# Reordering square sums, splits and copies in a two-block fp32 transformer kernel

## What is computed

```python
def first_block(x, ...):
    u = _rmsnorm(h, norm_mix_g[l])                       # first norm
    z = jnp.einsum('bsd,dn->bsn', u, w_in[l])
    q, k, v, pz, ga, gp = jnp.split(z, offs, axis=-1)
    a = _attention_branch(q, k, v)       # 12 heads of 64, dilated windows, dilation 1, 4, 16
    p = _pool_branch(pz, w_pool_grp[l], pool_scale[l])   # trailing means
    merged = sigmoid(ga) * (a @ w_att_out) + sigmoid(gp) * (p @ w_pool_out)
    h = h + merged @ w_out
    m = _rmsnorm(h, norm_mlp_g[l])
    h = h + jnp.square(jax.nn.relu(m @ w_mlp_in)) @ w_mlp_out
    return _rmsnorm(h, norm_final_g)

def second_block(x, ...):
    h = rms_norm(x, ln1_g[l]); z = h @ w_in[l] + b_in[l]
    q, k, v, u, y_branch, g_att, g_rec = jnp.split(z, SPLITS, axis=-1)
    y_att = neighbourhood_attention(q, k, v, rpb[l]) @ w_att_o[l]      # 8 heads of 64
    u = centred_depthwise_conv(u, conv_w[l], conv_b[l])
    h_fwd = rg_lru(u, ..., False); h_bwd = rg_lru(u, ..., True)        # gated recurrences
    y_rec = ((h_fwd + h_bwd) * gelu(y_branch)) @ w_rec_o[l]
    mixed = sigmoid(g_att) * y_att + sigmoid(g_rec) * y_rec
    x = x + mixed @ w_out[l]
    x = x + jnp.square(relu(rms_norm(x, ln2_g[l]) @ w_ff1[l])) @ w_ff2[l]
    return rms_norm(x, lnf_g)
```

## Time and profile before

| | |
|---|---|
| Timed executions | 2948.13, 2948.46, 2949.51 us; median 2948.46 us |
| The profiled execution's own time | 2945.8 us |
| Its span, first to last instruction | 2944.0 us |
| Mean granted clock of TensorE | 0.992 of full speed |
| TensorE busy | 2866.2 us, 97% of the span |
| VectorE, ScalarE, GpSimd busy | 1697.9, 1321.0, 209.5 us |
| Moved by DMA | 302.71 MB, mean 103 GB/s |

### The profile page before, as it was taken

How to read it: one execution, slowest core, us unless ns; L and a number is a source line. 1 busy time by engine, 2 the same in 40 slices (tenths; PEclk the granted TensorE clock), 3 DMA queues, 4 the chain that set the end, 5 groups by cost and what they waited for, 6 DMA issues and landing times.

```text
span 2944.0 us, 34460 instructions
## 1 busy us (share of the span) xinstructions
PE 2866.2 (97%) x13080; PEld 2272.9 (77%) x13080; DVE 1697.9 (58%) x2404; ACT 1321.0 (45%) x2120; POOL 209.5 (7%) x143
## 2 busy tenths in 40 slices
PE   7999999999999999999999999999999999999997
PEld 5777776888888878887666787777888888888885
DVE  4333356335866657687555523888334866666785
ACT  3444452113555544445344413788123555544452
POOL 4122420000000000000222200000000000000000
PEclk9999999999999999999999999999999999999998
DMA  3111111113334365432311111111114343384441
GB/s 115 37 37 36 37 36 47 54 51 122 126 150 150 147 256 211 162 118 68 123 51 51 44 50 57 50 58 45 56 36 152 128 150 150 132 316 159 154 133 57
DMA packets 84971, 302.71 MB, mean 103 GB/s; under 512 B 9424, under 2 KB 9552, under 8 KB 78544
## 3 DMA queue, kind: packets, MB, share of 16 engines
q1 hardware_dynamic: 83088, 294.31, 28.9%
q10 hardware_dynamic: 1728, 6.29, 0.7%
HBM read 225.07 MB, written 75.50 MB: 102 GB/s over the span
## 4 chain that ended last, share of the span: by engine, by line
PE 50%; issue 43%; DVE 4%; ACT 1%; POOL 1%; DMA 1%; SPq 0%; POOLq 0%; DVEq 0%; ACTq 0%
PE ps L2243 15%; PE ps L371 7%; PE ps L2511 5%; PE pa L2511 5%; PE ps L2540 4%; PE pa L2540 3%; PE ps L2387 2%; PE pa L2287 2%; PE ps L2556 1%; PE pa L2315 1%; PE pa L2296 1%; POOL sqsum L617 1%; DMA k_rraw<-hff 1%; DVE sm L1478 0%; PE pa L2202 0%
## 5 line engine op out<-in xcount | busy, mean ns | idle before, releaser
L361 DVE TENSOR_TENSOR w_lo<-w_raw,w_hi 128x1024 fp32r<-128x1024 f32 x134 | 161.7, 1208 | 475.7 <-ACT w_hi L355 475.7
L355 ACT ACTIVATE w_hi<-w_raw 128x1024 fp32r<-128x1024 f32 x134 | 137.9, 1030 | 464.7 <-PE ps L371 318.5
L371 PE MATMUL ps<-a_hi,w_hi 128*128 128x512 f32 x896 | 283.2, 397 | 6.0 <-DVE w_lo L361 4.4
L371 PE MATMUL ps<-a_hi,w_lo 128*128 128x512 f32 x896 | 281.9, 396 | 0.0
L371 PE MATMUL ps<-a_lo,w_hi 128*128 128x512 f32 x896 | 281.7, 396 | 0.0
L2243 PE MATMUL ps<-a_hi,w_hi 128*128 128x512 f32 x704 | 237.4, 418 | 22.6 <-DVE w_lo L361 10.3
L1140 ACT ACTIVATE krh<-k_rraw 128x512 fp32r<-128x512 f32 x192 | 121.0, 630 | 235.9 <-PE ps L2540 120.4
L2243 PE MATMUL ps<-a_hi,w_lo 128*128 128x512 f32 x704 | 225.6, 402 | 0.0
L2243 PE MATMUL ps<-a_lo,w_hi 128*128 128x512 f32 x704 | 225.4, 401 | 0.0
L1842 DVE TENSOR_TENSOR krl<-k_rraw,krh 128x512 fp32r<-128x512 f32 x192 | 132.5, 690 | 136.3 <-ACT krh L1140 136.0
L371 PEld LDWEIGHTS ps<-a_hi,w_hi 128*128 128x128 f32 x896 | 168.7, 190 | 49.6 <-issue 9.1
(11 more groups left out here) (323 smaller groups left out, 5968.5 us busy)
## 6 DMA issues: line engine op xcount, KB each, us to landing
w_raw<-wstream SPq DMA_DIRECT2D x134, 512.0 KB, 3.5
k_rraw<-hff SPq DMA_DIRECT2D x224, 256.0 KB, 2.7
hff<-hbuf SPq DMA_DIRECT2D x32, 1024.0 KB, 3.9
wA<-wff SPq DMA_DIRECT2D x16, 2048.0 KB, 7.9
hff<-hbuf SPq DMA_DIRECT2D x32, 768.0 KB, 3.3
w_raw<-wff SPq DMA_DIRECT2D x32, 512.0 KB, 4.1
f_raw<-wff SPq DMA_DIRECT2D x32, 512.0 KB, 4.4
hres<-zt SPq DMA_DIRECT2D x16, 512.0 KB, 2.6
```

What stands on the lines that cost most here:

```text
L355: nc.scalar.activation(w_hi[:, slot, 0:n], w_raw[:, slot, 0:n], ACT.Copy).then_inc(s_whi, 1)
L361: nc.vector.tensor_tensor(w_lo[:, slot, 0:n], w_raw[:, slot, 0:n], w_hi[:, slot, 0:n].bitcast(F32), ALU.subtract).then_inc(s_wlo, 1)
L371: mm = nc.tensor.matmul(out[0:m, c], w[0:kp, slot, wofs:wofs + m], x[0:kp, k, c * HC:(c + 1) * HC], start=first and n == 0, stop=last and ...
```

## The change

It does the following.
1. The first norm's squares are added by VectorE, not GpSimd; ScalarE takes w_hi of unit 0 first and the eight a_hi copies before the squares; w_hi and w_lo of unit 1 come among the squares. w_raw of unit 1 is loaded before the constants. `stats(0)` stands after step 84, the broadcast after step 114.
2. In attention 2 `v_out` goes between the two exps of a step.
3. In block 1's merge the splits of GA4 and the gate of GA3 change places with the row sums, the gates of GA6 and GA7 with a split each, and the first spread comes a k tile later.
4. In the recurrence `ur` is copied before w_hi is made; the split of mrg2's third unit moves ahead of `direction(7, 1)` and of the first three r_hi.

```diff
-SPREAD_AT = (1, 4, 6)
+SPREAD_AT = (2, 4, 6)
@@ SyncE
             for k in range(KT):
                 sp.dma_start(res[:, k], xT[k * P:(k + 1) * P]).then_inc(sem(f"s_big{k}"), 16)
+            load_unit(sp, 1, 1, True)
             sp.dma_start(cst[:], consts).then_inc(sem("s_cst"), 16)
-            load_unit(sp, 1, 1, True)
@@ GpSimd
-            for k in range(1, KT):
-                pool.wait_ge(sem("s_sq"), k + 1)
-                if k > 1:
-                    pool.wait_ge(sem("s_sqs"), k - 1)
-                nc.gpsimd.tensor_tensor(sqsum[:], sqsum[:], sq[:, k % 2], ALU.add).then_inc(sem("s_sqs"), 1)
@@ ScalarE, attention
                         exp(2 * s)
-                        exp(2 * s + 1)
+                        if b == 1:
+                            exp(2 * s + 1)
                     if p + 1 < npair and V_STEP[b] <= q < V_STEP[b] + VB[b]:
                         v_out(VB[b] * (p + 1) + q - V_STEP[b])
+                    if b == 2 and s < ns:
+                        exp(2 * s + 1)
@@ ScalarE, start
+            split_hi(act, 0, 0, 0, None)
             for k in range(KT):
                 act.wait_ge(sem(f"s_big{k}"), 16)
                 nc.scalar.activation(a_hi[:, k], res[:, k], ACT.Copy, scale=V("g_mix", k)).then_inc(sem("s_xh"), 1)
-                if k == 0:
-                    split_hi(act, 0, 0, 0, None)
+            square(0, 0)
+            square(0, 1)
+            split_hi(act, 1, 1, 0, None)
+            for k in range(2, KT):
                 square(0, k)
-            split_hi(act, 1, 1, 0, None)
@@ ScalarE, merge of block 1: before the three tanh of ga_t
+            unit_split(U_GA4)
...
-            unit_split(U_GA4)
@@ ScalarE, u_out
-                if c:
-                    split_hi(act, u + 2, u % 2, (u + 2) // 2, t + 1)
                 nc.scalar.activation(ur[c % 2][:, 2:2 + S], pair_flat(t), ACT.Identity, bias=V("b_in", 12 + c)
                                      ).then_inc(s_outA, 1)
-                if c == 0:
-                    split_hi(act, u + 2, u % 2, (u + 2) // 2, t + 1)
+                split_hi(act, u + 2, u % 2, (u + 2) // 2, t + 1)
@@ ScalarE, mrg2
+            split_hi(act, st.u + 2, st.u % 2, (st.u + 2) // 2, st.t + 1)
             for n in range(3):
                 rec_hi(n, REC_ORDER[n])
-            split_hi(act, st.u + 2, st.u % 2, (st.u + 2) // 2, st.t + 1)
@@ VectorE, start
+            split_lo(dve, 0, 0, None)
             for k in range(KT):
                 ...
-                if k == 0:
-                    split_lo(dve, 0, 0, None)
+            add_square(0, 1)
             split_lo(dve, 1, 1, None)
+            for k in range(2, KT):
+                add_square(0, k)
@@ VectorE, merge of block 1
-            unit_split(U_GA4)
-            gate(ga_t[3][:], T_GA3)
             dve.wait_ge(sem("s_rowc"), 6)
...
             link(nc.vector.tensor_tensor(lrow[:, 0], lrow[:, 0], lrow[:, 2], ALU.add))
+            unit_split(U_GA4)
+            gate(ga_t[3][:], T_GA3)
             link(nc.vector.reciprocal(mmin[:], lrow[:, 0]))
...
+            gate(ga_t[6][:], T_GA6)
             unit_split(U_GA7)
-            gate(ga_t[6][:], T_GA6)
...
             unit_split(U_AO1)
-            unit_split(U_GP)
             dve.wait_ge(sem("s_prod"), 4)
             gate(ga_t[7][:], T_GA7)
+            unit_split(U_GP)
@@ VectorE, recurrence and mrg2
                 gelu(c)
+                if c == KT - 1:
+                    split_lo(dve, st.u + 27, (st.u + 25) % 2, STAGES["mrg2"].t + 1)
                 direction(c, 1)
...
-            split_lo(dve, st.u + 2, st.u % 2, st.t + 1)
             for n in range(KT):
                 rec_lo(n, REC_ORDER[n])
@@ TensorE, attention(1)
+                    fill(48, 84)
                     stats(0)
-                    fill(48, 78)
+                    fill(84, 114)
                     broadcast(0)
-                    fill(78, 48 * 3)
+                    fill(114, 48 * 3)
```

## The result

The changed kernel took 2910.41 us, median of four runs (2908.9 to 2915.02), beside 2948.64 (2948.13 to 2949.51, four runs) for the kernel before: a ratio of 0.9873, 95% interval 0.9856 to 0.989. That is faster by 38.2 us, where 31.6 were summed and 2916.9 forecast. A second session measured the same two programs at 2949.46 and 2916.36 us (e5), 33.1 us apart.

The account below looks back on a forecast made before the run. TensorE, busy 97% of the span, was taken as the bound, leaving its waits and lower-clock time to gain. Terms of 12.5 + 6.0 + 2.0 + 6.4 + 3.9 + 0.8 = 31.6 us gave 2916.9 us, range 2911 to 2923.5.

Parts of the forecast that it names:

- Startup: First norm and units 0 and 1: unit 1 starts at 21.9 us, not 34.41, a gain of 12.5 us.
- Block 1's merge and the gates: Merge waits for plo and wrow go with a half-rate stretch, 6.0 us; gates of ga_t 6 and 7, 2.0 us.
- Attention 2: Twelve TensorE waits for the copy of v go, gaining 6.4 us (0 to 6.4).
- twelve times 0.53: Attention 2: twelve removed waits, each priced at its average of 0.53 us, give 6.4 us.
- Recurrence: Seven waits for ur nearly go, th is late next; net 0.55 us each, 3.9 us (3.0 to 5.8).
- Last gate units: mrg2: the 4.4 us wait goes, one of 3.5 us comes later; gain 0.8 us (0.5 to 2.5).
- I take the fall: Last gate units: the clock falls again behind the 3.5 us wait, taking 1.7 us off a gain of 2.5.
- Rival (c): All these waits go, the recurrence's too, and the clock stays up at the end: 35.2 us gained, 2913; chance 10%.
- (a): Startup: splits stay at 3.3 us without GpSimd's adds, so it gains about 1 us: 2928; chance 3%.
- (b): Attention 2: the value copy gives nothing, as the later second exp holds TensorE up: 2923; chance 6%.
- (d): Small queues taken as covered (sums, spreads, w_lo(1)) cost one or two us each: 2919 to 2924; chance 10%.
- (e): Startup: TensorE stays at 1.2 GHz after the first matmuls, through units 0 to 7; 2962 at 90 us; chance 2%.

Follow-up runs that it names:

- e5: The changed kernel again, no edit, in a second session: 2916.36 us against 2949.46 for the kernel before, ratio 0.9883.
- e2: The changed kernel with the seven square adds taken off VectorE and put back on GpSimd: 2924.82 us.
- e3: The kernel before with GpSimd's adds taken out and each square added by VectorE right behind its tile's split, old order kept: 2940.82 us.
- e11: The changed kernel with TensorE's sum back at step 48 and the broadcast at 78: 2921.47 us.
- e10: The changed kernel with VectorE's w_lo of GA4 and gate of GA3 back ahead of the row sums: 2916.47 us.
- e12: The changed kernel with the first spread back at k = 1: 2912.03 us.
- e6: The changed kernel with the recurrence's first tanh ahead of w_hi and mrg2's next split ahead of the r_lo: 2909.62 us against 2949.46, ratio 0.9859.
- e9: The changed kernel with mrg2's fourth unit's split ahead of the r_lo, timed: 2909.3 us against 2951.03 for the kernel before, ratio 0.9858.
- e1: The kernel before with only attention 2's value copies moved between the two exps: 2946.39 us against 2952.49, ratio 0.9976.
- e7: The changed kernel with the recurrence's first tanh ahead of the w_hi split in each round: 2909.65 us.
- e4: The changed kernel with the split of mrg2's third gate unit back behind direction(7, 1) and the r_hi: 2919.4 us.

## Why the prediction came out as it did

The direction held, and each wait that was named went or stayed as said. Three things were wrong: the price of a wait that goes, the cause of the merge's gain, and the fall of the clock at the end. The sum was 4.6 us short of the profiled span's 36.2.

**Startup**, 12.5 forecast, 12.4 measured. Splits at 1.28, one add before w_lo(1), six behind it, the sum at 30.4 where 30.3 was worked out: all as in the steps. Unit 1 began at 22.07 for 21.9. e2, e3 and e11 confirm that it takes the engine, the place of the adds and the place of the sum.

**Block 1's merge and the gates**, 8.0 forecast, 8.5 measured. All four waits and the half-rate stretch went. By position the merge gained 6.1 (forecast 6.0) and the gates 2.4 (forecast 2.0): the two gate waits were booked with 1.9 and took a restart of 0.25 each along. But the cause of the merge's part was put wrongly: I reckoned with VectorE's new order, and e10 shows that without it only 0.3 us is lost, since ScalarE's earlier w_hi and the later spread cover the rest. The 1.7 us for the clock were put on the two merge waits; e12, with the same stretch and neither wait, leaves open what brings it.

**Attention 2**, 6.4 forecast, 8.7 measured: the largest mis-sized term. "They end with the copy, wait no more" was right, "twelve times 0.53" was not: a wait that goes takes its restart along, 0.73 in all. I had set the row as an upper bound, and it was none.

**Recurrence**, 3.9 forecast, 3.4 measured. The wait fell from 0.83 to 0.28 us in seven rounds and th is late next, as said. The rounds gained 0.48 each, not 0.55.

**Last gate units**, 0.8 forecast, 2.35 measured. The moved wait of 3.4 us (forecast 3.5) is there; the step that failed is "I take the fall". Over all traces the clock fell behind the 3.2 to 3.4 us wait in five of seven executions (not in the first profile of the changed kernel, nor in e2) and behind the 4.4 us wait in four of four. The fall was the likelier case and not the one that the profiled execution met. Rival (c) had this half right; its other half, a recurrence without waits, did not come.

**First down product**, nothing forecast, 0.6 measured. A wait of 0.33 us for kll, whose neighbourhood the change does not touch, is missing in the changed kernel and back with 0.4 in e6 and e9: chance.

Together the misses are -0.1 + 0.5 + 2.3 - 0.5 + 1.55 + 0.6 = 4.35 of the 4.6; 0.2 lies behind the last gate units. Rivals (a) and (b) fell (e2, e1); of (d), no queue that was taken as covered cost anything; (e), a clock held down over the first units, did not show: the pairs were at full rate from 13.24 us. The range ended 0.6 us above the median, and with the restarts counted its low end would have been lower. The second session's median, 2916.36, lies in it, next to the forecast of 2916.9. That nearness is luck: the difference of 6 us between two sessions of one program is no part of any step. The one traced execution of that session has the slower spacing of matmuls told below, and the fall.

## What to carry to other kernels

A short wait of TensorE that goes altogether gives back its row plus the restart behind it (0.53 booked, 0.73 real in attention 2; 1.32 and 1.57 for plo), so many short waits are worth more than the list of waits says. One that only grows shorter does not: the recurrence's went from 0.83 to 0.28 and gave 0.48. When a split or a sum is late on one engine, look first at what its input stands behind on the other (e10), and before reordering copies ask whether the engine has too much in a row, for then the order only hands the wait on (e7). A reduction that TensorE reads in passing can be put behind all urgent work, but only if its reader is moved by as much (e11).

## What the hardware showed that was not expected

**Two spacings at one clock.** In the down products the same matmuls come about 229 ns apart in some executions and 233 in others, with a granted clock of 1.00 in both. The changed kernel's first profile:

```profile
1120.00:1300.00 180.00, 180.00 (x789) 147.67 (x788) 133.12 (x213) 83.19 (x142) 0.00 (x0) 1.00 0.48 151
2640.00:2840.00 200.00, 200.00 (x876) 164.13 (x875) 149.78 (x238) 95.98 (x160) 0.00 (x0) 1.00 0.46 142
```

and e5, the same program:

```profile
1120.00:1300.00 180.00, 180.00 (x773) 145.81 (x772) 128.75 (x207) 81.61 (x138) 0.00 (x0) 1.00 0.46 148
2640.00:2840.00 200.00, 200.00 (x859) 162.01 (x858) 148.05 (x238) 93.60 (x158) 0.00 (x0) 1.00 0.47 151
```

789 matmuls against 773 in 180 us is 2%, which makes some 5 us for each of the two stages. The first stage was slow in e1, e2 and e5, the second in e1, e4, e5, e6 and e10; in the other executions both were quick. No edit goes with it, and TensorE waits for nothing in these windows in either execution. It explains 9.4 of the 12 us by which the first profile and e5 differ; the fall behind the 3.4 us wait makes 1.6. Its cause is open.

**The fall is not settled by the wait.** Behind the wait of 3.4 us in the last gate units the granted clock went to 0.50 or stayed at 1.00 for one and the same program (e5). Behind waits of 3.2 to 4.4 us there, a stretch at half rate lasted 3.4 or 6.8 us, and 10.2 behind the 6.4 us of e2; and in e12 one came behind a wait of 0.8 us. A plan that leaves such a wait should reckon with either.
